# Three staging places of 2 MB for the next expert's gate/up weights, copied into their slots by GpSimd

## The chip, the cores and the metric

One core of a Trainium2 chip runs the whole kernel. The metric is the device time of one execution in microseconds. Before the change it was 1507.41 us, the median of three runs (1505.51 to 1507.91).

## What is computed

Two transformer layers over 256 tokens of width 1024, in float32. The first is a mixing layer (stick-breaking attention and gated linear attention) with a convolutional feed-forward; the second has a pooling mixer, latent attention and a mixture of experts. Only the last part matters here:

```python
N_EXPERTS = 32; TOP_K = 4; D_EXPERT = D_MODEL = 1024
logits = (ht @ w_router + b_router).astype(jnp.float32)
top_vals, top_idx = lax.top_k(logits, TOP_K)
...
def expert_block(args):
    xblk, e = args
    gu = xblk @ w_gate_up[e] + b_gate_up[e]          # w_gate_up[e]: 1024 x 2048 float32, 8 MB
    gate = jnp.minimum(gu[:, :D_EXPERT], SWIGLU_LIMIT)
    up = jnp.clip(gu[:, D_EXPERT:], -SWIGLU_LIMIT, SWIGLU_LIMIT)
    act = gate * jax.nn.sigmoid(SWIGLU_ALPHA * gate) * (up + 1)
    return act @ w_down[e] + b_down[e]               # w_down[e]: 1024 x 1024 float32, 4 MB
```

All 32 experts get tokens, so all 12 MB of each expert are read from HBM, 384 MB in total.

## The kernel before

**Stages.** The first layer and the second layer's attention stream their weights through a ring of six slots of 1 MB. Then comes the router, and then the experts. The work on experts is cut into jobs: a job is up to 64 tokens of one expert. An expert with more tokens has two jobs in a row. The tables of jobs (`job_expert`, `job_last`, ...) are computed on the chip, and `jobs_ready` tells the other engines that they stand; `job_last[e]` is the number of expert e's last job.

**Places.** An expert's weights lie in six places of 2 MB: four for the gate/up matrix, called pairs 0 to 3 (pairs 0 to 2 lie in `ring`, pair 3 in `ring_b`), and two for the down matrix (`ring_b`). There is one set of places for all experts. `pair_slot(g, pair)` is the tile of a place.

**Loads.** SyncE (SP) issues all weight loads in program order, so a load whose wait isn't over holds up all behind it. `load_gu(e, pair)` and `load_down(e, h)` issue one 2 MB load each. In the loop over experts (lines 386 to 397), the load of the next expert's pair 0, 1 or 2 waits on `gu_used`, which TensorE raises when it is through with that pair of the expert's last job; pair 3 waits on `gu_full` (gate/up of that job done); each half of the down matrix waits on `d_used`. Ahead of the loop stand the six loads of expert 0, each behind the last use of the ring slots that it overwrites.

**A job on TensorE** (`job_turn`): gate/up pairs 0 and 1 (L2000, 16 matmuls a pair), a piece of the previous job's combination (L2035), pair 2, another piece (L2035), pair 3, turning the next job's weights (L2022, L2024), gathering the next job's tokens (L1986), turning the activations (L2013), the next job's bias (L1843), and the down product (L2076, 32 matmuls, 16 on each 2 MB half). Between pair 3 and L2013 lies the activation function: VectorE takes the gate (L1418), ScalarE the sigmoid (L797), VectorE multiplies (L1420), takes the up half (L1422) and makes the product (L1426). The last job also adds the down bias (four matmul pairs at L2048).

**GpSimd** makes constants and a few small operations ahead of the experts and has nothing to do during them: its next instruction is L536, after the last job.

**Biases of the experts** are loaded from ScalarE's queue (L758, L760), behind the wait for the attention result `av1`. ScalarE's copy of them (L762) stands ahead of its part of the router in program order.

Of the kernel before, what the change touches and what calls it, by code (L numbers as in the profile page):

```python
# [26 lines left out]
F32R = mybir.dt.float32r  # L27
I32 = mybir.dt.int32
# [32 lines left out]
PAIRS = GU // 2  # L61

# [240 lines left out]
def sync_program(g, sp):  # L303
# [107 lines left out]
def gpsimd_program(g, pool):  # L411
# [120 lines left out]
    rsqrt("moe")  # L532

# [7 lines left out]
def scalar_program(g, act):  # L541
# [250 lines left out]
    def sigmoid(m, o):  # L792
# [4 lines left out]
        act.activation(t.sig[:], t.gate[:], ACT.Sigmoid, scale=SWIGLU_ALPHA).then_inc(s.sig_ready, 1)  # L797
# [42 lines left out]
def vector_program(g, dve):  # L840
# [573 lines left out]
    def swiglu(m, o):  # L1414
# [11 lines left out]
        dve.scalar_tensor_tensor(out=t.act[:], in0=t.up[:], scalar=1.0, in1=t.gate[:], op0=ALU.add,  # L1426
# [64 lines left out]
def tensor_program(g, pe):  # L1491
# [498 lines left out]
    def gate_up(m, o, e, pair):  # L1990
# [3 lines left out]
        pe.wait_ge(*expert_landed(g, e, 2 * pair))  # L1994
# [155 lines left out]
class Semaphores:  # L2150
    def __init__(self, new):
# [110 lines left out]
        self.out_ready = new("out_ready")  # L2262
        self.out_ready_act = new("out_ready_act")
# [19 lines left out]
class Buffers:  # L2283
# [95 lines left out]
    def attention(self, new):  # L2379
# [17 lines left out]
        self.v_tok = new("v_tok", [NB, MH, VD])  # L2397
        self.q_T = new("q_T", [MH, T])
        self.k_T = new("k_T", [MH, T])
        self.score = new("score", [MH, 384])  # L2400
        self.row_m = new("row_m", [MH, NB])
        self.row_l = new("row_l", [MH, NB])
        self.prob_T = new("prob_T", [MH, 384])
        self.y_pool = new("y_pool", [4, T])
        self.y_sq = new("y_sq", [4, T])
# [89 lines left out]
```

## Time and profile before

| | |
|---|---|
| median of 3 runs | 1507.41 us |
| the profiled execution, its own time | 1506.25 us |
| its span, first to last instruction | 1504.5 us |
| TensorE matmul busy | 1414.2 us (94%) |
| TensorE weight load busy | 776.5 us (52%) |
| VectorE busy | 584.1 us (39%) |
| ScalarE busy | 244.8 us (16%) |
| GpSimd busy | 97.6 us (6%) |
| moved by DMA | 480.70 MB |
| granted TensorE clock, mean | 0.994 |

The time before is 1.75 us more than the span, and the profiled execution is 1.2 us under the median. The experts run from about 550 us to 1490 us. "Busy" of TensorE says little there, since its matmuls overlap one another; what it waits for is read from the timeline. A DMA share of 9 tenths or more in a slice of the page means that the 16 DMA engines were never idle in it.

### The profile page before, as it was taken

To read this page: it belongs to the slowest core of one execution; us is meant where nothing else is said; L and a number is where in the kernel's file an instruction comes from. 1 tells how busy PE (TensorE), PEld (TensorE's weight loads), DVE (VectorE), ACT (ScalarE), POOL (GpSimd) and SP (SyncE) were. 2 spreads that over 40 slices of the span, in tenths; PEclk is the share of its full clock that TensorE was granted. 3 is DMA by queue.
4 is the path that set the end of the run, shared out by engine and by line. 5 is a ranking of instruction groups with operands and counts; after the bars stand their busy time and mean duration, and the time that the engine had idled before them with its cause. 6 is when DMAs were issued, how large, how long until landed. Compare 5 with 4: busy or idle time off the path is not lost.

```text
span 1504.5 us, 19806 instructions
## 1 busy us (share of the span) xinstructions
PE 1414.2 (94%) x7328; PEld 776.5 (52%) x7329; DVE 584.1 (39%) x1093; ACT 244.8 (16%) x420; POOL 97.6 (6%) x129
## 2 busy tenths in 40 slices
PE   7999999999989999999899999999899889989996
PEld 6768877999976664333334343343333334333332
DVE  2034744767654443333233333332232233323323
ACT  1223113344423320000001010010000001000001
POOL 3000011322216000000000000000000000000000
PEclk9999999999999999999999999999999999999998
DMA  8343334555543729999997999999999999999995
GB/s 272 115 155 125 112 114 162 173 181 182 172 131 133 297 95 428 428 427 429 428 429 292 427 428 429 427 429 427 429 427 428 430 427 429 427 429 428 428 428 223
DMA packets 77411, 480.70 MB, mean 320 GB/s; under 512 B 7019, under 2 KB 31272, under 8 KB 52808
## 3 DMA queue, kind: packets, MB, share of 16 engines
q1 hardware_dynamic: 73806, 476.79, 77.7%
q10 hardware_dynamic: 3578, 3.53, 0.8%
q8 instruction: 19, 0.31, 0.1%
q14 instruction: 8, 0.07, 0.0%
HBM read 479.26 MB, written 1.05 MB: 319 GB/s over the span
## 4 chain that ended last, share of the span: by engine, by line
PE 58%; DMA 37%; DVE 2%; issue 1%; ACT 1%; POOL 0%; SPq 0%; POOLq 0%; DVEq 0%; ACTq 0%
DMA ring<-in_w_gate_up 31%; PE bank L2000 16%; PE bank L1525 9%; PE bank L1759 8%; DMA ring_b<-in_w_gate_up 7%; PE bank L1535 7%; PE bank L2076 5%; PE bank L1771 4%; PE bank L1691 2%; PE bank L1986 1%; PE bank L2035 1%; PE bank L1843 0%; PE bank L1973 0%; PE bank L1916 0%; PE bank L2013 0%
## 5 line engine op out<-in xcount | busy, mean ns | idle before, releaser
L2000 PE MATMUL bank<-ring,x_T 128*64 128x512 f32 x1584 | 360.6, 599 | 42.4 <-DMA ring<-in_w_gate_up 42.0
L2000 PEld LDWEIGHTS bank<-ring,x_T 128*64 128x64 f32 x1584 | 107.1, 137 | 276.9 <-issue 186.0
L2076 PE MATMUL bank<-ring_b,act_T 128*64 128x512 f32 x1056 | 233.9, 595 | 0.5 <-ACT act_T L803 0.5
L1412 DVE TENSOR_TENSOR h<-h,bank 128x512 f32<-128x512 f32 x128 | 82.2, 683 | 292.5 <-PE bank L2035 292.3
L2076 PEld LDWEIGHTS bank<-ring_b,act_T 128*64 128x64 f32 x1056 | 72.8, 137 | 144.4 <-issue 132.3
L2000 PE MATMUL bank<-ring_b,x_T 128*64 128x512 f32 x528 | 120.5, 598 | 12.7 <-DMA ring_b<-in_w_gate_up 12.7
L1525 PE MATMUL bank<-x_nT,ring 128*128 128x256 f32 x512 | 113.7, 384 | 3.1 <-issue 3.1
L1525 PEld LDWEIGHTS bank<-x_nT,ring 128*128 128x128 f32 x512 | 98.0, 192 | 17.4 <-issue 3.9
L797 ACT ACTIVATE sig<-gate 128x512 f32<-128x512 f32 x33 | 20.8, 629 | 523.7 <-DVE gate L1418 523.7
L1759 PE MATMUL bank<-h_hi,ff_hi 128*128 128x256 f32 x352 | 99.8, 284 | 1.9 <-POOL h_lo L480 1.4
L1759 PE MATMUL bank<-h_lo,ff_hi 128*128 128x256 f32 x352 | 99.6, 283 | 0.0
L1759 PE MATMUL bank<-h_hi,ff_lo 128*128 128x256 f32 x352 | 99.6, 283 | 0.0
L1387 DVE SCALAR_TENSOR_TENSOR y_lo<-bank,slot_gate,y_hi 128x512 fp32r<-128x512 f32 x33 | 24.8, 751 | 190.9 <-ACT y_hi L783 190.9
L2000 PEld LDWEIGHTS bank<-ring_b,x_T 128*64 128x64 f32 x528 | 35.1, 136 | 83.4 <-issue 61.2
L1759 PEld LDWEIGHTS bank<-h_hi,ff_hi 128*128 128x128 f32 x352 | 67.5, 192 | 2.8 <-issue 1.7
L1986 PE MATMUL bank<-picks,h_half 128*128 128x128 f32 x512 | 68.1, 286 | 0.0
L1759 PEld LDWEIGHTS bank<-h_lo,ff_hi 128*128 128x128 f32 x352 | 67.5, 192 | 0.4
L670 ACT ACTIVATE ff_hi<-ring 128x2048 fp32r<-128x2048 f32 x33 | 61.8, 1903 | 35.5 <-DMA ring<-in_w_ffn_in 35.5
L1759 PEld LDWEIGHTS bank<-h_hi,ff_lo 128*128 128x128 f32 x352 | 67.5, 192 | 0.0
L536 POOL TENSOR_TENSOR bias_raw<-h,g_rows 128x1024 f32<-128x1024 f32 x1 | 2.4, 2353 | 955.9 <-DVEq L1479 955.9
L1986 PEld LDWEIGHTS bank<-picks,h_half 128*128 128x128 f32 x512 | 62.9, 196 | 0.8 <-issue 0.8
L473 POOL TENSOR_TENSOR ff_lo<-ring,ff_hi 128x2048 fp32r<-128x2048 f32 x11 | 51.1, 4641 | 159.0 <-PE bank L1759 111.3
(419 smaller groups left out, 1495.9 us busy)
## 6 DMA issues: line engine op xcount, KB each, us to landing
ring<-in_w_gate_up SPq DMA_DIRECT2D x96, 2048.0 KB, 25.5
ring_b<-in_w_down SPq DMA_DIRECT2D x64, 2048.0 KB, 23.0
ring_b<-in_w_gate_up SPq DMA_DIRECT2D x32, 2048.0 KB, 25.5
ring<-in_w_in SPq DMA_DIRECT2D x22, 1024.0 KB, 7.3
ring<-in_w_ffn_in SPq DMA_DIRECT2D x22, 1024.0 KB, 5.1
ring<-in_w_ffn_out SPq DMA_DIRECT2D x11, 1024.0 KB, 4.9
ring<-in_w_out SPq DMA_DIRECT2D x8, 1024.0 KB, 6.3
ring<-in_w_branch_sb SPq DMA_DIRECT2D x2, 1024.0 KB, 5.3
```

Of the source, the lines that this page charges most:

```text
L473: pool.tensor_tensor(t.ff_lo[:, 1, :], t.ring[:, slot, :], t.ff_hi[:, slot, :].bitcast(F32), ALU.subtract).then_inc(s.ff_lo_pool, 1)
L670: act.activation(t.ff_hi[:, n % RING, :], t.ring[:, n % RING, :], ACT.Copy).then_inc(s.ff_hi_done, 1)
L1387: dve.scalar_tensor_tensor(out=t.y_lo[:], in0=g.banks[4][:], scalar=t.slot_gate[:, 0:1], in1=t.y_hi[:].bitcast(F32), op0=ALU.mult, op1=ALU ...
L1412: dve.tensor_tensor(t.h[:, b, cols], t.h[:, b, cols], g.banks[2 + c][:], ALU.add).then_inc(s.added, 1)
L1525: ins = pe.matmul(bank[:, j * T:(j + 1) * T], wk[:, f * P:(f + 1) * P], src[:, k, :], start=(k == 0), stop=(k == len(weights) - 1))
L1535: ins = pe.matmul(bank[:, 0:n], src[:, k, b * P:(b + 1) * P], wk[:, c0:c0 + n], start=(k == 0), stop=(k == len(weights) - 1))
L1691: ins = pe.matmul(bank[:, q * T:(q + 1) * T], chunk(g, n, (4, 512))[:, k, P * (f % 4):P * (f % 4) + P], (t.o_sb, t.o_glaT)[q][:, k, :], st ...
L1759: ins = pe.matmul(bank[:, f * T:(f + 1) * T], wt[:, k, f * P:(f + 1) * P], ht[:, k, :], start=(k == 0 and part == 0), stop=(k == KT - 1 an ...
L1771: ins = pe.matmul(banks[2 * b + c][:], ut[:, q, k, b * P:(b + 1) * P], wt[:, k, 512 * c:512 * c + 512], start=False, stop=last, skip_group ...
L1986: ins = pe.matmul(banks[6][:, f * P:(f + 1) * P], t.h_half[:, b, k_rows], t.picks[:, b, :], start=(b == 0), stop=(b == 1))
L2000: ins = pe.matmul(banks[n][rows, :], t.x_T[:, c, :], job_slot(g, c)[:, c0:c0 + 512], start=False, stop=(c == GU - 1), skip_group_check=True)
L2076: ins = pe.matmul(banks[4][rows, :], t.act_T[:, k, SLOTS * (c // 2):SLOTS * (c // 2) + SLOTS], job_slot(g, GU + c)[:, c0:c0 + 512], start= ...
```

## The change

Three more places of 2 MB (`t.stage`) are added. The next expert's pairs 0, 1 and 2 are loaded into them, and GpSimd copies each into its slot (`tensor_copy`, 128 x 4096 float32) once the load has landed (`staged`) and the current expert's last job is through with the slot (`gu_used`). TensorE waits for the copy (`in_place`) where it waited for the load. Expert 0 is loaded straight into its slots as before, and expert 1's three staged pairs are loaded ahead of the experts, in the attention stage. Pair 3 and the down halves go straight to their places, as before. The order in which SP issues changes too. Some buffers of the attention and expert stages are put in another order in memory, and `gate` and `up` now lie in the memory of `bias_raw`.

```diff
+    def load_stage(e, pair):
+        sp.dma_start(t.stage[:, pair, :], gate_up[e, pair]).then_inc(s.staged[pair], 16)
...
     for h in range(2):
         load_down(0, h)
+    load_stage(1, 0)
     sp.wait_ge(*g.r2.filled("pp11"))
     load_gu(0, 1)
+    sp.wait_ge(*g.r2.filled("av1"))
+    load_stage(1, 1)
+    sp.wait_ge(*g.r2.filled("yt1"))
+    sp.wait_ge(s.msq_ready, NORM_AT["mla"] + 1)
+    load_stage(1, 2)
     sp.wait_ge(*g.r2.filled("pa11"))
     load_gu(0, 2)
...
+    def next_stage(m, pair):
+        sp.wait_ge(s.in_place[pair], m + 2)
+        load_stage(m + 2, pair)
+    def next_last_pair(m, last):
+        sp.wait_ge(s.gu_full, last * 2 + 2)
+        load_gu(m + 1, PAIRS - 1)
+    def next_down(m, last, h):
+        sp.wait_ge(s.d_used, last * DN + (2 * h + 2))
+        load_down(m + 1, h)
...
-    with sp.Fori(0, E - 1) as m:
-        last = sp.value_load(t.job_last[0:1, bass.ds(m, 1)], min_val=0, max_val=E + OVER - 1)
-        for pair in range(PAIRS):
-            if pair < PAIRS - 1:
-                sp.wait_ge(s.gu_used, last * (PAIRS - 1) + (pair + 1))
-            else:
-                sp.wait_ge(s.gu_full, last * 2 + 2)
-            load_gu(m + 1, pair)
+    last = last_job(0)
+    next_stage(0, 0)
+    next_stage(0, 1)
+    next_last_pair(0, last)
+    next_stage(0, 2)
+    for h in range(2):
+        next_down(0, last, h)
+    with sp.Fori(1, E - 2) as m:
+        last = last_job(m)
+        next_last_pair(m, last)
+        next_stage(m, 0)
         for h in range(2):
-            sp.wait_ge(s.d_used, last * DN + (2 * h + 2))
-            load_down(m + 1, h)
+            next_down(m, last, h)
+        next_stage(m, 1)
+        next_stage(m, 2)
+    last = last_job(E - 2)
+    next_last_pair(E - 2, last)
+    for h in range(2):
+        next_down(E - 2, last, h)
...
+    pool.wait_ge(s.jobs_ready, 1)
+    with pool.Fori(0, E - 1) as m:
+        last = pool.value_load(t.job_last[0:1, bass.ds(m, 1)], min_val=0, max_val=E + OVER - 1)
+        for pair in range(AHEAD):
+            pool.wait_ge(s.staged[pair], m * 16 + 16)
+            pool.wait_ge(s.gu_used, last * AHEAD + (pair + 1))
+            pool.sem_inc(s.place_free, 1)
+            pool.tensor_copy(pair_slot(g, pair), t.stage[:, pair, :]).then_inc(s.in_place[pair], 1)
...
-        pe.wait_ge(*expert_landed(g, e, 2 * pair))
+        if m is None or pair == PAIRS - 1:
+            pe.wait_ge(*expert_landed(g, e, 2 * pair))
+        else:
+            pe.wait_ge(s.in_place[pair], e + 1)
+        if m is None and pair < AHEAD:
+            pe.sem_inc(s.in_place[pair], 1)
```

The loop of SP over the experts, in the kernel before. Each `DMA` row is one 2 MB load, and the `ISA` row ahead of it holds its wait.

```order
L369 ISA [waits gu_used]
L369 DMA ring<-in_w_gate_up 128x4096
L390 REGISTER_ALU
L369 ISA [waits gu_used]
L369 DMA ring<-in_w_gate_up 128x4096
L390 REGISTER_ALU
L369 ISA [waits gu_used]
L369 DMA ring<-in_w_gate_up 128x4096
L392 ISA
L369 ISA [waits gu_full]
L369 DMA ring_b<-in_w_gate_up 128x4096
L395 ISA
```

Behind these rows stand the two down halves, each behind `d_used`. The first load of an iteration can go out when TensorE is through with the first pair of the expert.

The same loop after the change, from its first load.

```order
L370 ISA [waits gu_full]
L370 DMA ring_b<-in_w_gate_up 128x4096
L401 REGISTER_ALU
L373 ISA [waits in_place0]
L373 DMA stage<-in_w_gate_up 128x4096
L411 ISA
L376 ISA [waits d_used]
L376 DMA ring_b<-in_w_down 128x4096
L411 REGISTER_ALU
L376 ISA [waits d_used]
L376 DMA ring_b<-in_w_down 128x4096
L373 ISA [waits in_place1]
```

The first load of an iteration is now pair 3, behind `gu_full`, and the staged pairs 1 and 2 of the expert after the next close it.

GpSimd in the experts, after the change (before it, L536, there `bias_raw<-h,g_rows`, followed directly on the small operations ahead of the experts).

```order
L576 ISA [waits staged0]
L578 COPY ring<-stage 128x4096 [waits gu_used]
L576 REGISTER_ALU [waits staged1]
L578 COPY ring<-stage 128x4096 [waits gu_used]
L576 REGISTER_ALU [waits staged2]
L578 COPY ring<-stage 128x4096 [waits gu_used]
```

Three copies an expert stand where GpSimd had no instruction, one behind the other.

## Rows read from the trace of the kernel before

**Rows 1.** The page: DMA rate in 40 slices of 37.6 us.

```profile
GB/s 272 115 155 125 112 114 162 173 181 182 172 131 133 297 95 428 428 427 429 428 429 292 427 428 429 427 429 427 429 427 428 430 427 429 427 429 428 428 428 223
```

**Rows 2.** TensorE's waits from 575 to 1490 us: total, times, longest.

```profile
PE bank L2000 <- DMA ring<-in_w_gate_up: 42.0, 65, 1.2
```

**Rows 3.** Timeline of TensorE, a job without a wait for data.

```profile
574.58 7.09 PE L2076 MATMUL bank<-ring_b,act_T 128*64 128x512 f32 x32
...
600.80 7.09 PE L2076 MATMUL bank<-ring_b,act_T 128*64 128x512 f32 x32
...
615.35 3.65 PE L2000 MATMUL bank<-ring,x_T 128*64 128x512 f32 x16
```

**Rows 4.** Timeline of TensorE, the last job and the start of the one before.

```profile
1431.51 3.65 PE L2000 MATMUL bank<-ring,x_T 128*64 128x512 f32 x16 [0.20 <-DMA ring<-in_w_gate_up]
...
1460.89 3.65 PE L2000 MATMUL bank<-ring,x_T 128*64 128x512 f32 x16 [0.20 <-DMA ring<-in_w_gate_up]
...
1465.78 3.65 PE L2000 MATMUL bank<-ring,x_T 128*64 128x512 f32 x16 [0.19 <-DMA ring<-in_w_gate_up]
...
1471.09 3.65 PE L2000 MATMUL bank<-ring,x_T 128*64 128x512 f32 x16
...
1483.26 7.09 PE L2076 MATMUL bank<-ring_b,act_T 128*64 128x512 f32 x32 [0.47 <-ACT act_T L803]
```

**Rows 5.** Windows at the end: time, engines, clock, DMA share, GB/s.

```profile
1480.00:1485.00 5.00, 4.29 (x22) 2.14 (x22) 2.51 (x4) 1.10 (x4) 0.00 (x0) 1.00 0.83 351
```

**Rows 6.** Windows at the expert with two jobs.

```profile
796.00:798.00 2.00, 2.00 (x12) 0.61 (x10) 1.65 (x4) 0.00 (x0) 0.00 (x0) 1.00 0.12 49
...
806.00:808.00 2.00, 2.00 (x12) 0.72 (x10) 0.00 (x0) 0.00 (x0) 0.00 (x0) 1.00 0.55 106
808.00:810.00 2.00, 2.00 (x12) 0.58 (x8) 0.00 (x0) 0.00 (x0) 0.00 (x0) 1.00 0.78 287
```

**Rows 7.** Timeline of SP's issues: start, length, count, merged.

```profile
597.21 0.33 SPq L369 DMA_DIRECT2D ring_b<-in_w_gate_up  x1
...
806.48 8.00 SPq L369 DMA_DIRECT2D ring<-in_w_gate_up  x3
818.39 0.33 SPq L369 DMA_DIRECT2D ring_b<-in_w_gate_up  x1
```

**Rows 8.** One line of SP, 558 to 562 us: its first load of expert 1.

```profile
L369 SPq DMA_DIRECT2D ring<-in_w_gate_up x1: 348/348/348, 559.0 to 559.0; - x1
```

**Rows 9.** Timeline of TensorE around the expert's second job.

```profile
788.34 3.65 PE L2000 MATMUL bank<-ring_b,x_T 128*64 128x512 f32 x16 [0.58 <-DMA ring_b<-in_w_gate_up]
...
802.68 3.60 PE L2000 MATMUL bank<-ring,x_T 128*64 128x512 f32 x16
```

**Rows 10.** Windows ahead of the experts.

```profile
523.00:536.00 13.00, 13.00 (x43) 6.49 (x41) 5.14 (x6) 2.91 (x5) 0.00 (x0) 1.00 0.00 0
```

**Rows 11.** GpSimd's groups: operation, shapes, count, busy, mean ns.

```profile
L473 POOL TENSOR_TENSOR ff_lo<-ring,ff_hi 128x2048 fp32r<-128x2048 f32 x11 | 51.1, 4641 | 159.0 <-PE bank L1759 111.3 <-ACT ff_hi L670 47.7
...
L512 POOL CAST iota_s<-iota_i 128x128 f32<-128x128 int32 x1 | 0.3, 292 | 0.1
...
L510 POOL CAST iota_f<-iota_i 128x48 f32<-128x48 int32 x1 | 0.2, 228 | 0.1
```

**Rows 12.** Timelines of VectorE and TensorE in a job without a wait for data.

```profile
623.04 0.69 DVE L1420 TENSOR_TENSOR gate<-gate,sig 128x512 f32<-128x512 f32 x1 [0.77 <-ACT sig L797]
...
624.50 0.69 DVE L1426 SCALAR_TENSOR_TENSOR act<-up,gate 128x512 f32<-128x512 f32 x1
...
625.79 0.63 PE L2013 MATMUL bank<-ident,act 128*128 128x128 f32 x4
```

**Rows 13.** Timeline of ScalarE at the experts' biases.

```profile
518.45 1.76 ACTq L758 DMA_DIRECT2D bias_raw<-in_b_gate_up  x4
...
522.73 1.06 ACT L762 ACTIVATE bias_hl<-bias_raw 128x1024 fp32r<-128x1024 f32 x1 [9.94 <-DMA bias_raw<-in_b_gate_up]
531.67 1.09 ACT L575 ACTIVATE prob_T<-bank 128x512 f32<-128x512 f32 x2 [7.89 <-PE bank L1513]
```

More of the change, by code:

```diff
@@ L61 @@
 PAIRS = GU // 2
+AHEAD = PAIRS - 1
 VEC_A = dict(norm_mix=0, norm_ffn=8, attn_norm=16, ffn_norm=24, conv_w=32, conv_b=98, norm_end=120)
@@ L796, in sigmoid @@
             act.wait_ge(s.act_ready, nth(m, o, 1, 0))
[L797 removed]
+        act.activation(t.sig[:], t.gate, ACT.Sigmoid, scale=SWIGLU_ALPHA).then_inc(s.sig_ready, 1)
     def turned_act(m, o):
@@ L1425, in swiglu @@
             dve.wait_ge(s.act_turned, nth(m, o, 1, 0))
-        dve.scalar_tensor_tensor(out=t.act[:], in0=t.up[:], scalar=1.0, in1=t.gate[:], op0=ALU.add,
+        dve.scalar_tensor_tensor(out=t.act[:], in0=t.up, scalar=1.0, in1=t.gate, op0=ALU.add,
                                  op1=ALU.mult).then_inc(s.act_ready, 1)
@@ L2262, in __init__ @@
         self.out_ready = new("out_ready")
+        self.staged = [new(f"staged{n}") for n in range(AHEAD)]
+        self.place_free = new("place_free")
+        self.in_place = [new(f"in_place{n}") for n in range(AHEAD)]
         self.out_ready_act = new("out_ready_act")
@@ L2396, in attention @@
         self.k_tok = new("k_tok", [NB, MH, QK])
-        self.v_tok = new("v_tok", [NB, MH, VD])
         self.q_T = new("q_T", [MH, T])
         self.k_T = new("k_T", [MH, T])
-        self.score = new("score", [MH, 384])
+        self.v_tok = new("v_tok", [NB, MH, VD])
+        self.y_pool = new("y_pool", [4, T])
+        self.y_sq = new("y_sq", [4, T])
+        self.y_att = new("y_att", [NB, 512])
+        self.y_attn = new("y_attn", [NB, 512])
+        self.token_scale = new("token_scale", [T])
         self.row_m = new("row_m", [MH, NB])
         self.row_l = new("row_l", [MH, NB])
+        self.score = new("score", [MH, 384])
+        self.diag = new("diag", [NB, P])
+        self.iota_i = new("iota_i", [P], I32)
         self.prob_T = new("prob_T", [MH, 384])
-        self.y_pool = new("y_pool", [4, T])
-        self.y_sq = new("y_sq", [4, T])
-        self.diag = new("diag", [NB, P])
-        self.token_scale = new("token_scale", [T])
-        self.y_att = new("y_att", [NB, 512])
-        self.y_attn = new("y_attn", [NB, 512])
         self.ya_T = new("ya_T", [4, T])
         self.h_T = self.prob_T[:].rearrange("p h n -> p (h n)")[:, 0:KT * T].rearrange("p (k n) -> p k n", k=KT)
-        self.iota_i = new("iota_i", [P], I32)
         self.iota_f = new("iota_f", [JOBS])
@@ L2435, in experts @@
         self.ring_b = new("ring_b", [GU + DN - RING, CW])
-        self.x_T = new("x_T", [KT, SLOTS])
-        self.act_T = new("act_T", [4, P])
-        self.bias_hl = new("bias_hl", [FE], F32R)
-        self.bias_raw = new("bias_raw", [FE])
-        self.b_down = new("b_down", [D])
-        self.pos_T = new("pos_T", [T])
+        self.stage = new("stage", [AHEAD, 2 * CW])
+        self.bias_hl = new("bias_hl", [FE], F32R)
+        self.b_down = new("b_down", [D])
+        self.bias_raw = new("bias_raw", [FE])
+        self.gate, self.up = self.bias_raw[:, 0:512], self.bias_raw[:, 512:]
+        self.x_T = new("x_T", [KT, SLOTS])
         self.picks = new("picks", [NB, 2 * SLOTS])
-        self.x_part = new("x_part", [KT // 2, SLOTS])
-        self.h_half = new("h_half", [NB, 512])
-        self.bias_sel = new("bias_sel", [3 * SLOTS], F32R)
         self.mix_in = new("mix_in", [NB, 2 * SLOTS])
@@ L2449, in experts @@
         self.slot_gate = new("slot_gate", [1])
-        self.gate = new("gate", [512])
-        self.up = new("up", [512])
+        self.pos_T = new("pos_T", [T])
+        self.x_part = new("x_part", [KT // 2, SLOTS])
+        self.act_T = new("act_T", [4, P])
+        self.h_half = new("h_half", [NB, 512])
+        self.bias_sel = new("bias_sel", [3 * SLOTS], F32R)
         self.sig = new("sig", [512])
```

8 lines of the change are left out of this document (5 added, 3 removed).

## The prediction

> **What bounds the kernel now.** I read the page's DMA line first [rows 1]: from slice 16 on it stands at 427 to 430 GB/s, but for one slice of 292 and the last. So from 560 us to the end the DMA engines are the bound, except where they run dry. A 2 MB load (2.097 MB) takes 4.9 us at that rate, an expert's six loads 29.4 us. The waits of TensorE [rows 2] confirm it: 42.0 us in 65 waits for loads of pairs 0 to 2, none over 1.2 us. Then the timeline. A job that waits for no data takes 26.2 us from one down product to the next [rows 3]; late in the kernel a job takes 29.4 us (1431.51 to 1460.89) and its pairs start as they land, 4.89 us apart [rows 4]. TensorE alone would thus be 3.2 us a job faster than the loads.
>
> So the end is set by when the last load ends, and that by two things: the bytes left when the stream of loads starts, and the time in which it stands still. It starts when SP issues expert 1's first load at 559.0 [rows 8], and stands still once. At the expert with two jobs nothing may be overwritten until the second job is through with pair 0. The transfer ends at about 796.2 (2 us at 49 GB/s hold 0.2 us of work); SP issues at 806.48 [rows 7]; the slices from 806 fill as if the full rate began at 808.2 [rows 6], so from issue to bytes it is 1.7 us, and the engines are dry for 12.0 us. At the end they stop at about 1484.1 (351 of 428 GB/s in the window from 1480) [rows 5], and TensorE's last down product ends at 1490.4 [rows 4], 6.2 us behind.
>
> **The change, part by part, as the end of the stream moves.**
>
> 1. *Three loads ahead.* Expert 1's three staged pairs are loaded in the attention stage, where there is room: between 523 and 536 us nothing is moved [rows 10]. That takes 3 x 4.9 = **-14.7 us** from the stream. This is all that more places can win there.
>
> 2. *The stream starts later.* Its first load was free to go at 559.0. It is now a staged pair of expert 2, and its place must first be emptied by a copy that waits for the same `jobs_ready`. The trace has no copy of this size. Nearest are two conversions with one input, 128x48 in 228 ns and 128x128 in 292 ns [rows 11]: 0.8 ns an element, so 4096 elements take 3.5 us. The other bound is the two-input subtraction, 4641 ns for 2048 elements, so 9.3 us. I take 3.6 us with its start, since a copy is of the conversions' kind. **+3.5 us**. The next copies hide behind the load before them.
>
> The Trainium skill ("GPSIMD Engine Reference", section 3.1) puts a body with one input at 1.03 cycles an element, an estimate of 3.5 us for this copy; its 4497 ns for a two-input add stands beside the 4641 ns of the row. The sum would be the same by it.
>
> 3. *The queue runs dry once at the start.* Six loads can go before one that needs job 1: three of expert 2's stages, pair 3 and both down halves of expert 1. From 562.6 + 1.7, six loads end at 593.8. The next in SP's order is pair 3 of expert 2, behind `gu_full` of job 1, which before let its load out at 597.21 [rows 7], so bytes at 598.9: **+5.1 us**. TensorE has no lack in this time: it's full-buffer time, in which the lead just won is lost. From then on six loads a job (29.4 us) outlast TensorE's 26.2 us, and each wait of SP is over before its turn.
>
> 4. *The expert with two jobs.* Two more loads (staged pairs 1 and 2 of the next expert) stand ahead of the blocking one: -9.8 us. But that one is now pair 3, which waits for the second job's `gu_full` instead of the first pair: 818.39 against 806.48 [rows 7], +11.9 us. And TensorE gets to the second job earlier relative to the last down load: before, pair 3 started as it landed (788.34, two loads before 796.2, so 1.9 us behind its bytes) and the next job came 14.3 us later, 6.5 behind the last byte [rows 9]; with a staged load between pair 3 and the down halves it waits for the second down half instead, 1.9 us to landing and 3.5 us for its 16 matmuls, 5.4 behind. -1.1 us. Together **+1.0 us**: the lead of 6 MB buys nothing here.
>
> 5. *The tail.* Before, the last job's pairs 0 to 3 are the last loads but two, and its work runs beside them. Now two staged loads and pair 3 come behind the down half on which job 31 of 32 ends. With D the end of the last byte: that half ends five loads before D, lands 1.3 us later (the wait that ended at 1465.78 is for the load four before the last, 1484.1 - 19.6 = 1464.5) and takes 3.5 us, so the last job starts at D - 19.7. It takes 29.3 us without waits for data (1460.89 to 1490.4, less 0.19) [rows 4], and some 0.3 us for the copy of pair 1, whose load lands at D - 18.3 and is copied by D - 14.7. It ends at D + 9.9, against D + 6.2: **+3.7 us**.
>
> The sum is -14.7 + 3.5 + 5.1 + 1.0 + 3.7 = **-1.4 us**. The profiled execution goes from 1506.25 to 1504.9; it lies 1.2 us under the median, so against the median of 1507.4 the forecast is **1506.0 us**.
>
> *At nothing:* the 93 copies (335 us of GpSimd) lie where GpSimd had no work. In a job without waits the third copy starts as pair 2 ends (615.35 + 3.65 = 619.0) [rows 3] and ends at 622.7, before the next operation of VectorE with two inputs from SBUF at 623.04 [rows 12]. In a job bound by loads, copies hang on landings and can meet that operation, but 3.2 us of waits per job cover it. TensorE's waits are only renamed. The three early loads fit in front of the empty 13 us and into them [rows 10], and the first of them delays expert 0's pair 1 by 4.9 us, which isn't used before the experts.
>
> **Rivals.**
>
> - *Slower by the copies* (the other side). If a copy takes more than one load's 4.9 us, copies of pairs 1 and 2 queue: pair 2 is then in place 2c after pair 1 landed, at D - 18.3 + 2c, and from the start of pair 2 to the end it is 19.3 us (1471.09 to 1490.4) [rows 4]. For c = 6 the end is D + 13.0, 3 us worse than my tail, and the same lag once more at the two-job expert: 1512. For c = 9.3 both are 9.7: 1525. It decides from c = 5. For it: the two-input row; against: the one-input rows.
> - *Slower by VectorE.* A copy holds up VectorE's product at 623.04 or 624.50 [rows 12] in every job. L1426 ends at 625.2 and L2013 starts at 625.8, so 0.6 us is to spare, and a delay decides once it eats into the jobs' 3.2 us for more than a few jobs of the start, at some 2 us. With the whole 3.6 us a job takes 26.2 + 3.0 = 29.2 us; 32 jobs from 581.7 end at 1516, the last job's extras (29.3 - 26.2) make 1519, 29 us behind 1490.4: 1536. For it: the engines share their way to memory in no row that I have, so no row excludes it. The Trainium skill speaks for it ("SBUF — State Buffer", the reading of the diagram): GpSimd and a VectorE operation with two SBUF inputs lock each other out of a shared port pair for whole instructions. No row here shows it. Against: the copies lie clear of L1420 in jobs that set the pace.
> - *Slower by the biases.* The staged loads meet ScalarE's loads at 518.45 [rows 13], which had the engines nearly to themselves. The copy L762 at 522.73 may be later: ScalarE has 7.9 us of idle behind it. A longer delay shifts the router and all that follows by what is over: loads twelve us late instead of three would cost 1 to 5 us, 1507 to 1511.
> - *The lead is kept.* If SP's waits cost nothing at the start and the two-job expert, 14.7 us less 3.5: 1496; with the tail as before as well, 1492.5. Against: parts 3 and 4, which are waits in program order. A partial form, tail or second job cheaper than worked out, gives 1500 to 1503.
>
> **Numbers.** Forecast, within 1503 to 1509: 0.55. Copies slow: 0.10 (1510 to 1525). VectorE: 0.10 (1509 to 1536). Biases: 0.05 (1507 to 1511). Lead kept in part: 0.15 (1498 to 1503); kept whole: 0.05 (1492 to 1496). With 0.05 left out below and 0.12 above, the range is 1499 to 1514. 0.2% is 3 us, about what a measurement of this kernel tells from nothing: faster than 1504.4 is the kept lead and some of the forecast, 0.27; slower than 1510.4 is most of the three slow rivals, 0.22; within, 0.51.
>
> **What would show it.** The profile after should have: copies of 3.5 us at L578, 93 of them; a dry stretch of the DMA of 5 us at 594, one of 12 to 13 us at 805; a last byte about 5 us earlier than 1484.1 and a last down product some 10 us behind it. Wrong would be made by copies over 5 us, by L1420 waiting on them, by a router later than before, or by fewer dry microseconds.

## The result, and the profile after

The changed kernel takes 1514.41 us (median of 5, 1512.11 to 1515.80) against 1507.41 us (by now also of 5, 1505.51 to 1507.91). The ratio is 1.0048, 95% interval 1.0033 to 1.0062: slower by 0.5%, 7 us. The forecast was 1506.0 us, 1.4 us faster; the measured time lies just above its range and on the other side. The profiled execution is the quickest of the five, 1512.11 us with a span of 1510.4, so it stands against 1504.5.

The page of the changed kernel, the rate of the DMA by slices (now 37.8 us each), and the row of the copies.

```profile
GB/s 273 129 150 112 112 138 141 177 185 194 170 104 162 379 111 334 415 426 428 429 426 281 429 428 427 428 428 427 428 427 428 428 427 428 428 427 428 427 427 182
...
L578 POOL COPY ring<-stage 128x4096 f32<-128x4096 f32 x93 | 335.8, 3613 | 596.3 <-DMA stage<-in_w_gate_up 505.8
```

Against [rows 1] slice 14 has risen from 297 to 379: the lead was loaded. But slice 16 has fallen from 428 to 334: the stream started later than the forecast had it. The copies are as long as forecast, 3.6 us, 93 of them.

The cause stands ahead of the experts. The timeline of ScalarE, where the biases of the experts are loaded (it answers to [rows 13]), and the row of their landing; in the kernel before, that row reads 2.5/2.8/2.9.

```profile
516.41 1.77 ACTq L804 DMA_DIRECT2D bias_raw<-in_b_gate_up  x4
...
532.33 1.06 ACT L808 ACTIVATE bias_hl<-bias_raw 128x1024 fp32r<-128x1024 f32 x1 [21.57 <-DMA bias_raw<-in_b_gate_up]
```

```profile
DMA to landing us min/median/max: 8.1/11.1/14.6
```

From the first issue to the copy it is 15.9 us; before it was 4.3. Timelines show who waits for it, VectorE first, then TensorE (L1300 is the old L1254 and adds the attention's output product to `h`; L1559, the old L1513, turns `h` for the router; L1327 and L1581 are the old L1281 and L1535). The same places of the kernel before stand behind each.

```profile
522.44 0.75 DVE L1300 SCALAR_TENSOR_TENSOR h<-bank,rstd,h 128x512 f32<-128x512 f32 x1 [2.35 <-PE bank L1581]
533.41 1.22 DVE L1327 TENSOR_TENSOR bias_hl<-bias_raw,bias_hl 32x1024 fp32r<-32x1024 f32 x1 [10.22 <-ACT bias_hl L808]
534.66 0.75 DVE L1300 SCALAR_TENSOR_TENSOR h<-bank,rstd,h 128x512 f32<-128x512 f32 x1
```

```profile
525.25 1.22 DVE L1281 TENSOR_TENSOR bias_hl<-bias_raw,bias_hl 32x1024 fp32r<-32x1024 f32 x1
527.80 0.75 DVE L1254 SCALAR_TENSOR_TENSOR h<-bank,rstd,h 128x512 f32<-128x512 f32 x1 [1.34 <-PE bank L1535]
```

```profile
529.01 0.60 PE L1559 MATMUL bank<-ident,h 128*128 128x128 f32 x4
535.47 1.11 PE L1559 MATMUL bank<-ident,h 128*128 128x128 f32 x4 [5.86 <-DVE h L1300]
536.37 4.92 PE L1581 MATMUL bank<-ring,ya_T 128*128 128x512 f32 x8
...
581.01 7.09 PE L2127 MATMUL bank<-ring_b,act_T 128*64 128x512 f32 x32
```

```profile
531.91 3.60 PE L1535 MATMUL bank<-ring,ya_T 128*128 128x512 f32 x8
```

VectorE's first bias operation (L1327) stands between the first and the second of its four additions to `h`. While it waits for the bias, the additions behind it wait too, and TensorE with them. The first down product starts at 581.01, 64.6 us after the issue of the biases; before it was 574.58 and 518.45, so 56.1 us. The delay is 8.5 us. The profiled execution after was 2.0 us ahead at the issue, and already so at 455 us, before any of the change had run; so the span shows only 5.9 us.

The 8.5 us have three parts. *The wait:* ScalarE's copy comes 11.6 us later (15.9 - 4.3), and TensorE waits 5.9 us. The other 5.7 us are the cover, the time that passes before the delay reaches the engine that matters: 1.4 us before VectorE would have started L1327 in any case (10.2 us of wait there), 1.3 us that its second addition waited for TensorE before, and 3 us in which TensorE still had matmuls that don't need this addition. *The clock:* the granted clock falls in the wait and stands at 0.50, the lower of TensorE's two levels, from 533 to 539 us (the windows below). The eight matmuls of L1581 take 4.92 us instead of 3.60; with the four of L1559 ahead of them this costs 2.0 us.

```profile
531.00:533.00 2.00, 0.00 (x0) 0.00 (x0) 0.00 (x0) 0.68 (x1) 0.00 (x0) 0.80 1.07 348
533.00:535.00 2.00, 0.00 (x0) 0.00 (x0) 1.56 (x2) 0.86 (x2) 0.00 (x0) 0.50 0.82 332
...
537.00:539.00 2.00, 2.00 (x4) 0.74 (x3) 0.45 (x1) 1.36 (x3) 0.00 (x0) 0.50 0.00 0
```

*The rest,* 0.6 us, is not the biases': in the first job VectorE's product L1466 takes 1.25 us instead of 0.69 beside GpSimd's first copies. e2 below has it too.

**The terms of the sum, read from the trace.** The first two rows below are SP's first loads of the stream and its first load after the second job of the expert with two (they answer to [rows 7, 8]); then come the windows around its dry stretch and at the end [rows 5, 6], the last down product [rows 4], and GpSimd's first three copies. The sum of these terms is called the ledger from here on.

```profile
570.58 3.87 SPq L373 DMA_DIRECT2D stage<-in_w_gate_up  x2
...
822.60 0.34 SPq L370 DMA_DIRECT2D ring_b<-in_w_gate_up  x1
```

```profile
810.00:812.00 2.00, 2.00 (x12) 0.59 (x10) 0.00 (x0) 0.00 (x0) 1.36 (x1) 1.00 0.66 279
...
822.00:824.00 2.00, 2.00 (x17) 1.68 (x16) 1.74 (x3) 0.60 (x3) 0.00 (x0) 1.00 0.64 123
824.00:826.00 2.00, 2.00 (x18) 1.67 (x16) 0.33 (x1) 0.40 (x2) 0.00 (x0) 1.00 0.67 238
...
1485.00:1490.00 5.00, 4.29 (x22) 1.95 (x20) 2.67 (x4) 1.73 (x5) 0.00 (x0) 1.00 0.23 98
```

```profile
600.00:602.00 2.00, 2.00 (x10) 0.58 (x9) 1.41 (x3) 0.00 (x0) 2.00 (x1) 1.00 0.83 352
602.00:604.00 2.00, 2.00 (x14) 0.89 (x10) 1.19 (x3) 0.63 (x1) 1.00 (x1) 1.00 0.06 25
604.00:606.00 2.00, 2.00 (x18) 2.00 (x18) 1.37 (x2) 0.45 (x2) 0.00 (x0) 1.00 0.82 172
606.00:608.00 2.00, 2.00 (x14) 1.08 (x14) 0.21 (x1) 0.66 (x2) 0.00 (x0) 1.00 0.89 377
```

```profile
1489.16 7.09 PE L2127 MATMUL bank<-ring_b,act_T 128*64 128x512 f32 x32 [0.47 <-ACT act_T L849]
```

```profile
566.67 10.96 POOL L578 COPY ring<-stage 128x4096 f32<-128x4096 f32 x3 [22.36 <-issue]
```

| term | forecast | measured | how |
|---|---|---|---|
| three loads ahead | -14.7 | -14.7 | 3 x 4.9 at the measured rate; not measured apart |
| stream starts later, against the first down product | +3.5 | +5.2 | 570.58 - 581.01 against 559.0 - 574.58 |
| dry near the start | +5.1 | +3.7 | 601.7 to 605.4 |
| two-job expert | +1.0 | +1.0 | 811.3 to 824.3, 13.0 against 12.0 |
| tail | +3.7 | +3.9 | 1486.1 to 1496.25, 10.1 against 6.2 |
| first down product later | 0 | +8.5 | above |
| sum | -1.4 | +7.6 | medians +7.0; span +5.9, and 2.0 of head start |

The points in time come from the windows as before: 279 of 428 GB/s in the 2 us from 810 are 1.3 us of work, and so on. All terms but the last hold to 1.7 us, and the two that are off make up for one another. GpSimd's first copy began at 566.67, 1.2 us later than the load that it stands in for would have gone out (559.0 + 6.4, by the two down products), and SP's load went out 0.3 us behind its end; so the six loads behind it ended later, and the dry stretch was shorter.

### The profile page after: what moved, and what is told of

The parts are those of the page before. It is cut to its first block, busy times and chain, and to the rows that moved or that the text cites. A ratio compares the mean times of both kernels' runs of the same rounds, so it can differ in the third digit from the quotient of the medians.

```text
span 1510.4 us, 20213 instructions
## 1 busy us (share of the span) xinstructions
PE 1414.6 (94%) x7328; PEld 781.0 (52%) x7329; DVE 689.7 (46%) x1093; ACT 244.9 (16%) x420; POOL 433.4 (29%) x223
## 4 chain that ended last, share of the span: by engine, by line
PE 45%; DMA 43%; POOL 6%; DVE 3%; issue 1%; ACT 1%; SPq 0%; POOLq 0%; ACTq 0%; DVEq 0%
DMA stage<-in_w_gate_up 40%; PE bank L1571 8%; PE bank L1805 8%; PE bank L2051 6%; PE bank L1581 6%; POOL ring L578 6%; PE bank L1817 4%; PE bank L2127 4%; PE bank L1737 2%; DMA ring_b<-in_w_down 2%; DMA bias_raw<-in_b_gate_up 1%; PE bank L2086 1%; PE bank L2032 1%; DVE bias_raw L1466 0%; PE bank L2019 0%
## 5 line engine op out<-in xcount | busy, mean ns | idle before, releaser
L578 POOL COPY ring<-stage 128x4096 f32<-128x4096 f32 x93 | 335.8, 3613 | 596.3 <-DMA stage<-in_w_gate_up 505.8
L843 ACT ACTIVATE sig<-bias_raw 128x512 f32<-128x512 f32 x33 | 20.8, 629 | 490.7 <-DVE bias_raw L1464 490.7
L1466 DVE TENSOR_TENSOR bias_raw<-bias_raw,sig 128x512 f32<-128x512 f32 x33 | 62.5, 1894 | 25.4 <-ACT sig L843 25.4
L1372 DVE TENSOR_SCALAR mix_in<-iota_s,job_pos 128x128 f32<-128x128 f32 x64 | 73.9, 1196 | 0.0
```

The source lines that it names most:

```text
L578: pool.tensor_copy(pair_slot(g, pair), t.stage[:, pair, :]).then_inc(s.in_place[pair], 1)
L1372: dve.tensor_scalar(t.mix_in[:, b, :], t.iota_s[:], pos(b), None, ALU.is_equal).then_inc(s.mix_in_ready, 1)
L1466: own(dve.tensor_tensor(t.gate, t.gate, t.sig[:], ALU.mult))
```

## Experiments

Times are medians. The kernel before was run beside each group, on the same chip: 1506.74 us in the group of e1 to e4, 1508.13 us in e5 to e8, 1507.94 us in e9 to e11, 1507.63 us for e12.

### e1: the loads alone

It has the changed kernel's early loads and memory layout, with the loop, GpSimd and TensorE of before. Against the changed kernel:

```diff
-    pool.wait_ge(s.jobs_ready, 1)
-    with pool.Fori(0, E - 1) as m:
...
-            pe.wait_ge(s.in_place[pair], e + 1)
+        pe.wait_ge(*expert_landed(g, e, 2 * pair))
```

> The kernel before the change in its loop of loads, its waits of TensorE and its idle GpSimd, but with the memory layout of the changed kernel and with the three staged loads of expert 1 issued in the attention stage; nothing reads them, so 6 MB are moved for nothing. Theory (the biases' loads from ScalarE's queue are held up by the staged loads, and with them the router): the biases land 10 us or more after their issue, as in the changed kernel (14.6 us), TensorE stands still for about 6 us after the first half of the attention's output product, and the whole is 7 to 9 us slower than before, 1515 to 1516 us. Rival (the loss comes from the copies, the new order of SP or VectorE's waits for GpSimd): as before, 1507 us.

Measured: 1514.82 us, ratio 1.0047 (1.0031 to 1.0062). The biases' copy waited for them again, and TensorE behind it (L1542 is here what L1559 is there).

```profile
  DMA bias_raw<-in_b_gate_up: 20.3, 1
...
DMA to landing us min/median/max: 6.8/10.3/13.3
```

```profile
536.19 1.11 PE L1542 MATMUL bank<-ident,h 128*128 128x128 f32 x4 [4.62 <-DVE h L1283]
```

ScalarE's copy starts 14.7 us after the first issue, 10.4 us later than before, and TensorE waits 4.6: the cover is 5.8 us again. The early loads by themselves cost 8 us, with no copy, no new order and no new wait. The rival is out.

### e2: two early loads issued after the biases

```diff
     sp.wait_ge(*g.r2.filled("av1"))
-    load_stage(1, 1)
     sp.wait_ge(*g.r2.filled("yt1"))
     sp.wait_ge(s.msq_ready, NORM_AT["mla"] + 1)
-    load_stage(1, 2)
     sp.wait_ge(*g.r2.filled("pa11"))
     load_gu(0, 2)
+    load_stage(1, 1)
+    load_stage(1, 2)
```

> The changed kernel with one edit: the staged pairs 1 and 2 of expert 1 are issued behind the load of expert 0's pair 2, that is after the biases have landed and the router's input is made, and before the experts begin. Theory of the biases: the 8.4 us of the router come back, the other terms of the forecast stand, 1506 us. Rival (the copies and the order cost the 7 us): 1514 us, as the changed kernel. A third: the staged pair 0 and expert 0's pair 1, still in front of the biases, delay them in part: 1507 to 1511 us.

Measured: 1506.15 us, ratio 0.9992 (0.9982 to 1.0002). The ledger without its last term says -0.9 us, the medians -0.6. The biases landed after 3.9 to 4.9 us, and ScalarE's copy came 7.4 us after the first issue:

```profile
519.50 3.34 ACTq L804 DMA_DIRECT2D bias_raw<-in_b_gate_up  x4
...
526.85 1.06 ACT L808 ACTIVATE bias_hl<-bias_raw 128x1024 fp32r<-128x1024 f32 x1 [13.01 <-DMA bias_raw<-in_b_gate_up]
```

That is 3 us later than before and moved nothing. VectorE waited 1.7 us for it and TensorE not at all, as the cover of 5.7 us wants it. The cover is set by VectorE's program order, not by ScalarE's idle time of 7.9 us.

### e3: VectorE's products out of GpSimd's way

With e2's order of loads. This kernel leaves out the clamps at 7.

```diff
-        own(dve.tensor_tensor(t.gate, t.gate, t.sig[:], ALU.mult))
+        own(dve.tensor_tensor(t.gate, g.banks[0][:], t.sig[:], ALU.mult))
...
-        dve.scalar_tensor_tensor(out=t.act[:], in0=t.up, scalar=1.0, in1=t.gate, op0=ALU.add,
+        dve.scalar_tensor_tensor(out=t.act[:], in0=g.banks[1][:], scalar=1.0, in1=t.gate, op0=ALU.add,
```

> The kernel of e2_late, but VectorE's two products in the activation function take the gate and the up half from PSUM instead of from the clamped copies in SBUF, so no operation between gate/up and down reads two tensors from SBUF. This leaves the clamps at 7 out of the product. Theory (VectorE's product is held up by a copy of GpSimd in the jobs bound by loads, and it is covered by their 3.2 us): L1466 falls from 1.9 us to 0.7 us on average, and the time stays within 1 us of e2_late. Rival (the held-up products cost time): 2 to 5 us faster than e2_late.

Measured: 1506.36 us, ratio 0.9994 (0.9981 to 1.0007): as e2. The row of the product (L1466) in e2, and in e3:

```profile
L1466 DVE TENSOR_TENSOR bias_raw<-bias_raw,sig 128x512 f32<-128x512 f32 x33 | 62.5, 1894 | 25.5 <-ACT sig L843 25.5
```

```profile
L1466 DVE TENSOR_TENSOR bias_raw<-bank,sig 128x512 f32<-128x512 f32 x33 | 22.8, 692 | 25.5 <-ACT sig L843 25.5
```

With two inputs from SBUF it took 1.2 us longer on average than the 0.69 us of the kernel before [rows 12], and one input from PSUM cures it. The Trainium skill ("SBUF — State Buffer", the reading of the diagram) has GpSimd and such an operation lock each other out; by these rows the trace agrees. In this order of loads it costs nothing: TensorE's waits for the product fall from 24.7 us in 22 jobs to nothing, and its waits for the copies grow from 29.7 to 46.5 us.

### e4: staged pair 0 ahead of pair 3

Against e2:

```diff
     with sp.Fori(1, E - 2) as m:
         last = last_job(m)
+        next_stage(m, 0)
         next_last_pair(m, last)
-        next_stage(m, 0)
```

> The kernel of e2_late, with the staged pair 0 issued ahead of pair 3 in the loop of SP, so that it doesn't stand behind gu_full. Theory (dry stretches of the DMA come from the program order of SP's waits): the stretch of 3.7 us near the start shrinks to about 1.3 us, the 13 us at the expert with two jobs become about 11.5 us in pieces, the tail stays at 10 us, together 3.4 us faster than e2_late. Rival (SP's order is not what holds the DMA): no change.

Measured: 1535.89 us, with executions from 1514.37 to 1551.88. The three quickest (1514.37, 1528.36, 1532.26) give the ratio 1.0190 (1.0156 to 1.0225). The granted clock of the six is 0.965 to 0.981; the kernel before, run beside it, has 0.990 to 0.996. Neither theory had this. The profile is of the 1514.37, 8 us over e2; what the longer executions lost beyond that no trace shows. Timelines of TensorE, VectorE and GpSimd in one job:

```profile
626.75 0.85 PE L2064 MATMUL bank<-ident,act 128*128 128x128 f32 x4 [1.90 <-DVE act L1472]
627.54 1.22 PE L1889 MATMUL bank<-bias_hl,bias_sel 64*128 64x512 f32 x4
628.69 8.04 PE L2127 MATMUL bank<-ring_b,act_T 128*64 128x512 f32 x32
```

```profile
621.95 3.30 DVE L1466 TENSOR_TENSOR bias_raw<-bias_raw,sig 128x512 f32<-128x512 f32 x1 [0.77 <-ACT sig L843]
```

```profile
621.11 3.60 POOL L578 COPY ring<-stage 128x4096 f32<-128x4096 f32 x1 [7.10 <-DMA stage<-in_w_gate_up]
```

and windows of the same stretch:

```profile
625.00:627.00 2.00, 0.24 (x2) 0.25 (x3) 1.63 (x3) 0.00 (x0) 0.99 (x1) 1.00 1.08 459
627.00:629.00 2.00, 2.00 (x10) 1.10 (x11) 1.36 (x2) 0.66 (x2) 2.00 (x1) 0.56 1.02 434
629.00:631.00 2.00, 2.00 (x8) 0.49 (x6) 1.97 (x3) 0.00 (x0) 1.16 (x1) 0.58 0.97 410
```

The copy runs from 621.11 to 624.71. The product (L1466), due at 621.95, ends 0.5 us behind the copy's end (0.69 us is its own length). TensorE stands still for 1.9 us, and then its granted clock is at 0.56 to 0.58 for some 4 us, near the lower of its two levels of 1.2 and 2.4 GHz; the down product takes 8.04 us instead of 7.09 [rows 3]. Over this execution TensorE waits 37.9 us in 20 jobs before L2064. In 13 of them the down product behind the wait (1.9 to 2.6 us) takes 7.9 to 8.8 us; in jobs without one, and in the changed kernel, whose waits there reach 1.2 us, it is 7.09. This is the prediction's rival of VectorE, brought on by when the copies fall, and the clock behind the stall was not in its price.

### e5 and e6: two cures for it

e5 computes the reference with one operand from PSUM in each product; e6 leaves VectorE as it is and cuts the copies.

e5 against the kernel of e4:

```diff
-        own(dve.tensor_tensor(t.gate, t.gate, t.sig[:], ALU.mult))
+        own(dve.scalar_tensor_tensor(out=t.gate, in0=g.banks[0][:], scalar=SWIGLU_LIMIT, in1=t.sig[:], op0=ALU.min,
+                                     op1=ALU.mult))
...
-        dve.tensor_scalar(t.up, g.banks[1][:], SWIGLU_LIMIT, -SWIGLU_LIMIT, ALU.min, ALU.max)
+        dve.tensor_scalar(g.banks[1][:], g.banks[1][:], SWIGLU_LIMIT, -SWIGLU_LIMIT, ALU.min, ALU.max)
-        dve.scalar_tensor_tensor(out=t.act[:], in0=t.up, scalar=1.0, in1=t.gate, op0=ALU.add,
+        dve.scalar_tensor_tensor(out=t.act[:], in0=g.banks[1][:], scalar=1.0, in1=t.gate, op0=ALU.add,
```

e6 against the kernel of e4:

```diff
-            pool.tensor_copy(pair_slot(g, pair), t.stage[:, pair, :]).then_inc(s.in_place[pair], 1)
+            for q in range(4):
+                part = slice(q * 2 * CW // 4, (q + 1) * 2 * CW // 4)
+                pool.tensor_copy(pair_slot(g, pair)[:, part], t.stage[:, pair, part]).then_inc(
+                    s.in_place[pair] if q == 4 - 1 else s.place_free, 1)
```

> The kernel of e4_late_order, with VectorE's two products taking one operand from PSUM: the first is min(bank, 7) times the sigmoid in one operation, and the clamped up half is written back to its bank. It computes the reference. Theory (in e4_late_order copies of GpSimd met VectorE's product, TensorE stood still for 1.9 us in such jobs, and its clock then fell): L1466's successor takes 0.7 us, TensorE's waits before L2064 vanish, the granted clock goes back from 0.98 to 0.994, and the gain of the order worked out before shows, 1502 to 1504 us. Rival (the order itself costs the time, by when loads land): 1514 us or more, as e4_late_order.

> The kernel of e4_late_order with each copy of GpSimd cut into four of 1024 columns, the last of which raises in_place; VectorE's products as they were. Theory (a product waits for the copy under way and not for bandwidth): L1466 waits at most for one quarter, 0.9 to 1.1 us, its mean stays under 1.5 us, TensorE's clock holds at 0.99, 1503 to 1506 us. Rival (VectorE stands in line behind all of GpSimd's queued copies, or shares a bandwidth): L1466 stays at 1.9 us or more on average, and the time at 1514 us or more.

Measured: e5 1502.24 us, ratio 0.9959 (0.9944 to 0.9974); e6 1502.36 us, ratio 0.9962 (0.9949 to 0.9975). Both are faster than the kernel before by 6 us, and, going by the ratios, than the changed one by 13 us and than e2 by 4.5 to 5 us (3.4 had been worked out for the order). The two products in e5:

```profile
L1466 DVE SCALAR_TENSOR_TENSOR bias_raw<-bank,sig 128x512 f32<-128x512 f32 x33 | 22.8, 691 | 25.4 <-ACT sig L843 25.4
...
L1473 DVE SCALAR_TENSOR_TENSOR act<-bank,bias_raw 128x512 f32<-128x512 f32 x33 | 22.8, 691 | 1.1
```

and the product in e6, 0.74 us long with two inputs from SBUF:

```profile
L1469 DVE TENSOR_TENSOR bias_raw<-bias_raw,sig 128x512 f32<-128x512 f32 x33 | 24.3, 738 | 25.5 <-ACT sig L846 25.5
```

So the order was right, and either cure of the hold, with the clock that hangs on it, takes away the whole of e4's loss. What VectorE waits for is the copy under way, not a share of bandwidth: in e6 the same bytes are copied.

### e7: every copy twice

With e2's order of loads and e5's products:

```diff
-            pool.tensor_copy(pair_slot(g, pair), t.stage[:, pair, :]).then_inc(s.in_place[pair], 1)
+            for half in range(2):
+                pool.tensor_copy(pair_slot(g, pair), t.stage[:, pair, :]).then_inc(s.half_copies if half == 0 else s.in_place[pair], 1)
+                if half == 0:
+                    pool.wait_ge(s.half_copies, m * AHEAD + (pair + 1))
+                    pool.sem_inc(s.place_free, 1)
```

> The kernel of e2_late with every copy of GpSimd made twice, so that a place takes about 7.3 us to empty, and with the products of e5_order_exact, so that the copies hold up nothing of VectorE's there. Theory (the rival of slow copies, as priced in the prediction): the last job's pair 2 starts at D - 18.3 + 2c, the tail grows by 5 us, the wait at the expert with two jobs by 5 us, the stream starts 3.6 us later: 1519 to 1521 us. Rival (copies are hidden by the loads): under 1510 us.

Measured: 1532.70 us, ratio 1.0155 (1.0137 to 1.0173), above both. Here other operations of VectorE met the copies. Its timeline in one job (four small `picks` operations, 0.73 us for all four in e4, took 7.5 us), and TensorE's next step:

```profile
1317.08 7.50 DVE L1370 TENSOR_SCALAR picks<-iota_s,job_pos 128x64 f32<-128x64 f32 x4
```

```profile
1326.04 0.68 PE L2091 MATMUL bank<-y_hi,spread 64*128 64x512 f32 x2 [3.16 <-DVE h L1462]
```

The four end with GpSimd's copies (1313.46 to 1324.53). They have one input, from SBUF, and so has a 128x2 copy ahead of them that took 3.57 us. So operations with one input from SBUF can be held as well. TensorE's waits for VectorE's additions that follow, total, times, longest (e12 has none of them):

```profile
PE bank L2091 <- DVE h L1462: 60.4, 22, 5.0
```

### e8: the change without its lead

Against e2:

```diff
-    load_stage(1, 0)
...
     load_gu(0, 2)
-    load_stage(1, 1)
-    load_stage(1, 2)
...
+    for pair in range(AHEAD):
+        load_stage(1, pair)
     last = last_job(0)
```

> The kernel of e2_late without the lead: expert 1's three staged pairs are loaded when the table of jobs stands, as before the change, and not in the attention stage. What is left of the change are the copies and the order. Theory (the ledger of loads): the stream has 14.7 us more to load, but starts 5 us earlier, at 559, and never runs dry near its start (3.7 us), so against e2_late it is 6 us slower, 1512 us. Rival (the lead of 6 MB is worth its whole 14.7 us): 1521 us. Another (the lead is worth nothing): 1506 us.

Measured: 1512.26 us, ratio 1.0032 (1.0020 to 1.0045). That is 6 us over e2: of the 14.7 us of loads that the lead takes away, 6 us reach the end. The rest goes where the ledger says. SP's first load of the stream goes out 39.5 us after the issue of the biases, in e2 44.7, so 5.2 us earlier; and the rate near the start stays at 418 to 442 GB/s where the others have the dry stretch (3.7).

### e9: short rows for the early loads

Against the changed kernel, whose order of loads it keeps; the load of pair 2 is cut in the same way.

```diff
+    def load_stage_short(e, pair):
+        for q in range(4):
+            part = slice(1024 * q, 1024 * q + 1024)
+            sp.dma_start(t.stage[:, pair, part], gate_up[e, pair][:, part]).then_inc(
+                s.staged[pair] if q == 3 else s.short, 16)
...
-    load_stage(1, 1)
+    load_stage_short(1, 1)
...
+    pool.wait_ge(s.short, 16 * 6)
```

> The changed kernel with one edit: the staged pairs 1 and 2 of expert 1, in their old place ahead of the biases, are each loaded by four transfers of 1024 columns (rows of 4 KB on each partition, as the biases' rows are) instead of one with rows of 16 KB. Theory (the DMA engines take the two queues in turn by pieces that follow the row, so that with 16 KB rows on SP's queue ScalarE's queue gets about a fifth of the rate): the biases get near to half of the rate and land in 5 to 8 us instead of 14.6, the router is late by 1 to 3 us, 1507 to 1510 us. Rival (what is queued first on SP's queue goes first, or ScalarE's queue is slow for another reason): 14 us to landing and 1514 us, as the changed kernel.

Measured: 1507.07 us, ratio 0.9997 (0.9989 to 1.0006). The biases landed sooner, the last just above the 5 to 8 us that were expected, and the time is at the lower edge:

```profile
DMA to landing us min/median/max: 5.1/6.9/8.3
```

The bytes, their place and the start of their issue are the same, the rows are shorter, and 7 us of the loss are gone. 8.3 us is 5.4 later than before, inside the cover of 5.7. (The profiled execution is one of the slowest, 1510.7 us, with the clock at 0.50 around the issue, so TensorE's waits in it say little.) So the loss hangs on how the early loads are cut, not on their bytes. The edit makes four transfers of 512 KB out of one as well, and SP takes 6.3 us to issue them instead of 4.1; which of the two decides, the row or the transfer, was not tested, nor by what rule the engines take the queues in turn.

### e10 and e12: a later release without a longer hold

Both with e2's order of loads and e5's products; the edit as in e10, in e12 the 90 is a 44.

```diff
-            pool.tensor_copy(pair_slot(g, pair), t.stage[:, pair, :]).then_inc(s.in_place[pair], 1)
+            pool.tensor_copy(pair_slot(g, pair), t.stage[:, pair, :]).then_inc(s.copied, 1)
+            pool.wait_ge(s.copied, m * AHEAD + (pair + 1))
+            for _ in range(90):
+                pool.sem_inc(s.place_free, 1)
+            pool.sem_inc(s.in_place[pair], 1)
```

> The kernel of e2_late with VectorE's products taking an operand from PSUM (as in e5_order_exact), and with GpSimd raising 90 semaphore counts between the end of each copy and in_place, so that a place takes longer to empty while nothing more is read or written. It separates what e7_twice_exact mixed: the later release and the longer hold on VectorE. Let c be copy plus signal, about 7.2 us if one count takes 40 ns. Theory (e7's excess of 12 us over its price was VectorE waiting for the second copies, and TensorE's clock behind it): L1366's four small operations stay near 0.2 us each or wait for one copy at most, the granted clock stays at 0.99, and the time is that of the ledger, 1519 to 1521 us at c = 7.2, and 3.7 us less or more for each us of c. Rival (the late release alone costs it): 1530 us or more.

> The kernel of e10_slow_signal with 44 counts instead of 90. In e10 the next copy started 7.47 us after a copy's end, so a count takes 83 ns, c was 11.1 us, and GpSimd itself was the bound at 34 us an expert; with 44 counts c is 7.25 us and an expert 22 us of GpSimd. Theory (the ledger with c = 7.25 and a hold on VectorE of 3.6 us a copy as in e2_late): 1519 to 1521 us, granted clock 0.99. Rival (the late release alone accounts for e7_twice_exact): 1530 to 1535 us.

Measured: e10 1679.56 us, ratio 1.1142 (1.1127 to 1.1156). The size was wrong: a count takes 83 ns, not 40, and three times 11 us are more than an expert's 29.4 us of loads, so GpSimd set the pace. It decides nothing on e7. e12 took 1519.43 us, ratio 1.0075 (1.0062 to 1.0088), as priced; its granted clock, 0.974 in the profile, fell more than expected. So a release 3.65 us later costs 13 us over e2. The windows of e12 at the expert with two jobs and at the end, and its last down product, show where:

```profile
808.00:810.00 2.00, 2.00 (x12) 0.67 (x10) 0.00 (x0) 0.00 (x0) 0.00 (x0) 1.00 0.33 139
...
828.00:830.00 2.00, 2.00 (x19) 2.00 (x19) 1.07 (x2) 0.42 (x2) 0.00 (x0) 1.00 0.93 213
830.00:832.00 2.00, 2.00 (x13) 0.91 (x14) 0.57 (x2) 0.66 (x2) 1.72 (x1) 1.00 0.98 418
...
1490.00:1495.00 5.00, 5.00 (x24) 1.64 (x22) 2.32 (x4) 0.00 (x0) 0.00 (x0) 1.00 0.18 75
```

```profile
1499.54 7.09 PE L2132 MATMUL bank<-ring_b,act_T 128*64 128x512 f32 x32 [0.47 <-ACT act_T L853]
```

The DMA is dry for 20.4 us (808.65 to 829.05), in e2 for 13.1; the tail is 15.8 us (1490.9 to 1506.6), in e2 10.0. Near the start it is not dry at all, so there the later start costs nothing. e7 takes 12 us more than e12 by the ratios. The two differ in what fills the time, a second copy or counts; in e7 the `picks` operations take 1.27 us on average, in e12 0.46. So these 12 us are what the second copies held up.

### e11: both cures

The kernel of e5 with the copies of e6:

```diff
-            pool.tensor_copy(pair_slot(g, pair), t.stage[:, pair, :]).then_inc(s.in_place[pair], 1)
+            for q in range(4):
+                part = slice(q * 2 * CW // 4, (q + 1) * 2 * CW // 4)
+                pool.tensor_copy(pair_slot(g, pair)[:, part], t.stage[:, pair, part]).then_inc(
+                    s.in_place[pair] if q == 4 - 1 else s.place_free, 1)
```

> The kernel of e5_order_exact with the copies of e6_order_split, four parts each. Theory (either cure alone removes the stall of TensorE, so both together bring nothing more): 1501.5 to 1503.5 us, L1372 down from 1.1 us to under 0.7. Rival (what is left of the waits between VectorE and GpSimd still costs time): 1499 to 1501 us.

Measured: 1502.64 us, ratio 0.9965 (0.9954 to 0.9977): no more than either alone. The second sign missed: `mix_in` (L1372, here L1375), another operation with one input from SBUF, still takes 0.82 us on average, not under 0.7.

## Why the prediction was wrong

**The step that failed is the rival of the biases, mispriced and given 0.05.** The prediction named the place (ScalarE's loads at 518.45 beside the staged loads) and the sign ("a router later than before"), and went wrong in three ways. It gave a long delay 0.05 without a reason; the biases landed up to 14.6 us after their issue instead of 2.9, because of the early loads beside them (e1) and of how these are cut (e9). It took the cover from the wrong engine: ScalarE's 7.9 us of idle instead of the 5.7 us that VectorE's program order leaves, since the old L1281 stands between the additions that TensorE waits for. And it put TensorE's clock behind the wait at nothing. By the prediction's own rule a copy 11.6 us late costs 11.6 - 7.9 = 3.7 us, inside its 1 to 5; measured are 5.9 us of wait and 2.0 us of lower clock. By "at nothing" the prediction also let the early loads pass, for they fit into idle time of the DMA; that they fit says nothing of what else is in the queue in that time. e1 shows that this part alone gives the whole loss, e2 that without it the rest of the sum holds.

**The ledger of loads was right.** Its sum of -1.4 us stands beside -0.9 by the measured terms and -0.6 us in e2. Parts 4 and 5 hold to 0.2 us; parts 2 and 3 are off by +1.7 and -1.4 us. They are one term in two places, since a later start takes from the dry stretch behind it, so that the sum came out is not luck. Part 1 was not measured apart, but e8 confirms what the lead is worth after parts 2 and 3, 6 us.

**The price of a copy was right**, 3.6 us, and the estimate by the Trainium skill ("GPSIMD Engine Reference", section 3.1) of 3.5 us with it. The rival of slow copies, not met in the changed kernel, had its price about right too. For c = 7.25 the prediction's formula, D + 1.0 + 2c against D + 9.9, gives 5.6 us at the tail and as much at the two-job expert, 11.2 us; it leaves out the later start, which costs nothing while there is a dry stretch to take it from. e12 against e2 gave 13 us: 5.8 at the tail, 7.3 at the two-job expert.

**VectorE's rival** was real and cost nothing here, as worked out for jobs bound by loads: L1466 was 1.9 us long on average, TensorE waited up to 1.2 us before L2064, 24.7 us in 22 jobs, and e3 took these waits away for no gain. Its price, 1509 to 1536, put the clock at nothing: in e4 the granted clock was at 0.56 to 0.58 behind a stall of 1.9 us, and executions went up to 1552.

## What to carry to other kernels

An early load that fits into idle DMA time still stands beside other queues: look for small loads on the same engines in that time, and for who is behind their consumer in program order on each engine, not only on the one that waits first. More buffer is worth what it takes from the stream, less each wait of the issuing queue that now blocks on something later; here a ledger of dry stretches of the DMA found each such term to 1.7 us and the sum to 1 us. When an engine waits in a stretch that was full, price the clock of TensorE behind the wait too. In this kernel a GpSimd copy of 3.6 us held VectorE operations on SBUF until it ended; cutting it into four, or giving VectorE a PSUM operand, cured it.

## What the runs showed of the hardware that was not expected

- How long a small load takes beside a large one on another DMA queue hangs on how the large one is cut: 0.5 MB of biases landed after 14.6 us at the latest beside 2 MB loads with 16 KB rows, after 8.3 us beside the same bytes in four loads each with 4 KB rows, and nearly alone after 2.9 us.
- A GpSimd copy of 3.6 us holds a VectorE operation with two inputs from SBUF to its end (3.30 us instead of 0.69), and in e7, under copies back to back, small ones with one SBUF input as well (7.5 us for four instead of 0.73). The two products with one operand from PSUM are not held (0.69 us on average over 33).
- After TensorE had waited 1.9 us, its granted clock was 0.56 to 0.58 for about 4 us (e4). In the changed kernel's wait of 5.9 us it fell to 0.50, and stayed there for 3.5 us after work began again.
- A semaphore count on GpSimd took 83 ns (90 of them 7.47 us, e10).
